# The sample gates of a hybrid decoder step: products with ones in place of a transpose and selection products

## What is computed

```python
g_nsa = jax.nn.sigmoid(nsa_g.reshape(bsz, t, N_HEADS, 3))
o_nsa = jnp.einsum('bthk,btkhd->bthd', g_nsa, o_br).reshape(bsz, t, Q_DIM)
```

## Time and profile before

| | us |
|---|---|
| median of 3 runs | 2087.87 |
| fastest and slowest of them | 2085.74, 2093.57 |
| span of the profiled execution | 2092.6 |
| TensorE busy in it | 2026.6 |
| VectorE, ScalarE, GpSimd busy | 425.8, 323.0, 115.4 |

### The profile page before, as it was taken

One profiled execution on the slowest core, in us unless ns is written; L12 is line 12 of the kernel. 1 busy time (PEld: TensorE's weight loads), 2 busy tenths in 40 slices (PEclk: granted clock), 3 DMA queues, 4 the chain that ended last, 5 costly groups with the idle time before them and its releaser, 6 DMA issues.

```text
span 2092.6 us, 40370 instructions
## 1 busy us (share of the span) xinstructions
PE 2026.6 (97%) x17044; PEld 1201.8 (57%) x17044; DVE 425.8 (20%) x1129; ACT 323.0 (15%) x852; POOL 115.4 (6%) x215
## 2 busy tenths in 40 slices
PE   8998999999999999899999999999999999999996
PEld 6776677777777778567777443343434343434332
DVE  1234365210000132437431300000000000000001
ACT  2243221110000123522211110000101000001010
POOL 2210121000000010120000000000000000000000
PEclk9999999999999999999999999999999999999998
DMA  8852653334333364453333699999999999999996
GB/s 321 301 197 97 209 183 142 141 121 141 136 126 141 118 222 154 150 202 132 116 122 121 259 419 404 414 384 417 378 421 392 409 392 408 390 409 390 408 396 258
DMA packets 98441, 551.25 MB, mean 263 GB/s; under 512 B 12992, under 2 KB 29408, under 8 KB 39520
## 3 DMA queue, kind: packets, MB, share of 16 engines
q1 hardware_dynamic: 84144, 492.75, 60.5%
q0 software_dynamic: 12112, 48.93, 6.6%
q10 hardware_dynamic: 2016, 7.08, 0.9%
HBM read 532.84 MB, written 22.13 MB: 265 GB/s over the span
## 4 chain that ended last, share of the span: by engine, by line
PE 52%; issue 43%; DVE 2%; ACT 1%; DMA 1%; POOL 1%; POOLq 0%; DVEq 0%; SPq 0%
PE bank L463 41%; PE bank L594 3%; PE bank L624 1%; PE bank L649 1%; ACT phase_region L1216 1%; PE bank L841 1%; PE bank L711 1%; PE bank L733 1%; PE bank L777 0%; DVE phase_region L1612 0%; POOL xn L1193 0%; PE bank L637 0%; PE bank L482 0%; PE bank L474 0%; PE bank L563 0%
## 5 line engine op out<-in xcount | busy, mean ns | idle before, releaser
L982 PE MATMUL bank<-wring,phase_region 128*32 128x512 f32 (+2 forms) x9728 | 871.1, 519 | 3.0 <-DMA wring<-in_wstream 2.0
L463 PE MATMUL bank<-xn,wring 128*128 128x288 f32 x2496 | 643.6, 418 | 5.7 <-DVE phase_region L1612 3.6
L982 PEld LDWEIGHTS bank<-wring,phase_region 128*32 128x32 f32 x9728 | 311.5, 110 | 557.4 <-issue 510.3
L463 PEld LDWEIGHTS bank<-xn,wring 128*128 128x128 f32 x2496 | 481.5, 195 | 148.3 <-issue 10.9
L1216 ACT ACTIVATE phase_region<-bank 128x384 f32<-128x384 f32 (+14 forms) x244 | 87.9, 442 | 420.2 <-PE bank L947 205.3
L463 PE MATMUL bank<-phase_region,wring 128*128 128x288 f32 x608 | 148.2, 407 | 3.1 <-DVE mark L1540 2.5
L463 PEld LDWEIGHTS bank<-phase_region,wring 128*128 128x128 f32 x608 | 115.3, 190 | 36.0 <-DVE mark L1540 3.4
L2085 DVE TENSOR_TENSOR tmp<-phase_region,bank 128x512 f32<-128x512 f32 x32 | 22.0, 687 | 531.5 <-PE bank L982 531.5
L1494 ACT ACTIVATE phase_region<-bank 128x512 f32<-128x512 f32 (+1 forms) x48 | 25.2, 543 | 524.7 <-PE bank L982 524.7
L2098 DVE COPY phase_region<-bank 32x256 f32<-32x256 f32 x32 | 13.4, 420 | 297.5 <-PE bank L982 297.2
L594 PE MATMUL bank<-pages,wring 128*64 128x128 f32 (+1 forms) x1024 | 58.9, 276 | 0.0
(11 more groups left out here) (332 smaller groups left out, 1145.7 us busy)
## 6 DMA issues: line engine op xcount, KB each, us to landing
wring<-in_wstream SPq DMA_DIRECT2D x449, 1024.0 KB, 7.7
pages<-in_cmp_pages POOLq DMA_DIRECT2D x64, 128.0 KB, 3.7
pages<-in_cmp_pages SPq DMA_DIRECT2D x64, 128.0 KB, 3.6
pages<-in_slc_pages SPq DMA_DIRECT2D x64, 128.0 KB, 4.6
pages<-in_slc_pages POOLq DMA_DIRECT2D x64, 128.0 KB, 4.6
out_win_keep<-in_win_rows POOLq DMA_DIRECT2D x2, 4064.0 KB, 26.1
y_rows<-phase_region ACTq DMA_DIRECT2D x18, 384.0 KB, 8.1
pages<-in_win_kT POOLq DMA_DIRECT2D x4, 1024.0 KB, 5.3
```

The source lines that it names most:

```text
L463: mm = nc.tensor.matmul(ps[:, 0:width], wb, rhs(k), start=(k == 0), stop=(k == n - 1))
L982: mm = nc.tensor.matmul(ps[QT * q:QT * q + QT, 0:n], lhsT, w, start=start, stop=stop)
```

## The change

The constant `gate_sel` goes, and with it 1536 columns of the constants. The transpose, its bank, its copy on ScalarE and the signal `gT_ready` go. In their place VectorE, right after the norm of the layer and ahead of the rotation, waits for `gates_ready` and makes `gX` in the area of `o_ssm`, which is free at that time. For each group g it is one multiplication: 32 partitions (token t'), 384 columns (branch k, r, token t), the value being the gate (k, r) of token t' where t = t' and zero elsewhere, which is the gate times an identity. TensorE, at the old place of the twelve products, multiplies `gX[:, g]` with a 32 x 64 block of ones into partition half g: the sum over t' leaves the gate of token t on all 64 partitions. These are two matmuls of 384 columns. The copy to `gB` (L1299) and everything behind it stay as they are.

```diff
--- before.py
+++ after.py
@@ -132,12 +132,6 @@
     c["stack"] = (i[:, None] % QT == np.arange(QT)[None, :]).astype(np.float32)
     c["before"] = (i[:, None] < i[None, :]).astype(np.float32)
     c["exp_rank"] = np.broadcast_to(NE - np.arange(NE, dtype=np.float32), (P, NE))
-    sel = np.zeros((P, 12, P), np.float32)
-    for br in range(3):
-        for r in range(GRP):
-            for g in range(NKV):
-                sel[(g * GRP + r) * 3 + br, br * GRP + r, g * HD:(g + 1) * HD] = 1
-    c["gate_sel"] = sel.reshape(P, -1)
     return c
 
 
@@ -227,8 +221,8 @@
         vtok = ra(3, 3, P)
         gates = ra(3, 24)
         small = ra(3, 32)
-        gT = ra(TS)
         gB = ra(3, GRP, TS)
+        gX = view(oS_, 0, NKV, 3 * GRP * TS)
 
         kvT = [(ra(HALF, NCS), ra(HALF, NCS)), (view(oC_, 0, HALF, NCS), view(oC_, HALF * NCS, HALF, NCS))]
         kcTp, vcTp = ra(NCP + 1), ra(NCP + 1)
@@ -340,7 +334,7 @@
         pg_full = [sem(f"pg_full{i}") for i in range(6)]
         names = ("const_in par_in tables_in x_in0 x_in1 ptab_in sq_ready xn_ready x_ready small_ready gates_ready qkv_ready qksq_ready "
                  "inv_ready qkinv_ready rot_in0 rot_in1 rot_cos qk_ready vtok_ready vcT_ready vc_ready smax exp_ready norm_ready pt_ready "
-                 "qbd_ready scmax sc_exp pc_ready ptc_ready ssmax ss_exp pts_ready orow_ready gT_ready attn_done "
+                 "qbd_ready scmax sc_exp pc_ready ptc_ready ssmax ss_exp pts_ready orow_ready gX_ready attn_done "
                  "st_in xbcc_raw xbcc_ready cols_ready spa sp_exp ea_ready dD_ready eb_ready seg_ready dec_exp "
                  "dec_ready tl_sub tl_ready cp_ready xdt_ready btok_ready h_ready bm_ready y_ready ysq_ready "
                  "oS_ready part_sum merged_ready cnt_ready pick_ready table_ready zero_ready "
@@ -524,16 +518,12 @@
                 mm.then_inc(done, 1)
                 for i in range(2, 5):
                     product(("in", l, i), KD, lambda k: xn[:, k, :])
-                pe.wait_ge(S["gates_ready"], l + 1)
-                ps, done = bank(("gT", l))
-                nc.tensor.transpose(ps[0:24, 0:TS], gates[0:TS, 2, :], C("ident", TS)[:, 0:TS]).then_inc(done, 1)
                 for i in range(5, 8):
                     product(("in", l, i), KD, lambda k: xn[:, k, :])
-                pe.wait_ge(S["gT_ready"], l + 1)
+                pe.wait_ge(S["gX_ready"], l + 1)
                 ps, done = bank(("gB", l))
-                for j in range(12):
-                    mm = nc.tensor.matmul(ps[:, j * TS:(j + 1) * TS], C("gate_sel", 24)[:, j * P:(j + 1) * P],
-                                          gT[0:24, :], start=True, stop=True)
+                for g in range(NKV):
+                    mm = nc.tensor.matmul(ps[HD * g:HD * g + HD, 0:3 * GRP * TS], C("ones", TS)[:, 0:HD], gX[0:TS, g, :], start=True, stop=True)
                 mm.then_inc(done, 1)
                 product(("in", l, 8), KD, lambda k: xn[:, k, :])
                 ps, done = bank(("qkss", l))
@@ -1288,10 +1278,6 @@
                 A.activation(gates[:, 0:2, :], small[:, 0:2, 0:24], ACT.Sigmoid).then_inc(S["gates_ready"], 1)
                 for i in range(2, 5):
                     qkv_tile(i)
-                act.wait_ge(*filled(("gT", l)))
-                ps = bank_of(("gT", l))
-                copy(gT[0:24, :], ps[0:24, 0:TS]).then_inc(free(("gT", l)), 1)
-                signal("gT_ready")
                 for i in range(5, 8):
                     qkv_tile(i)
                 act.wait_ge(*filled(("gB", l)))
@@ -1565,6 +1551,13 @@
                 rms(l, 0, "norm_mix")
                 if l == 0:
                     dve.wait_ge(S["tables_in"], 16)
+
+                dve.wait_ge(S["gates_ready"], l + 1)
+                for g in range(NKV):
+                    mine = gates[0:TS, 2, 12 * g:12 * g + 12].rearrange("p (r k) -> p k r", k=3)
+                    one = bc(bc(C("ident", TS)[:, 0:TS], 1, GRP), 1, 3)
+                    last = V.tensor_tensor(gX[0:TS, g, :].rearrange("p (k r t) -> p k r t", k=3, r=GRP), bc(mine, 3, TS), one, ALU.mult)
+                last.then_inc(S["gX_ready"], 1)
 
                 for part, (i0, i1) in enumerate(ROT_PARTS):
                     dve.wait_ge(S[("rot_in0", "rot_in1")[part]], 64 * (l + 1))
```

## The result

| | before | changed |
|---|---|---|
| median of 7 runs, us | 2087.87 | 2080.32 |
| lowest and highest | 2085.58, 2093.83 | 2078.38, 2084.82 |
| span of the profiled execution | 2092.6 | 2077.7 |
| mean granted clock in it | 0.983 | 0.987 |

The ratio is 0.996, with a 95% interval of 0.9947 to 0.9972: 7.6 us of 2087.9, 0.36%. The forecast was 2080.0 us, within 0.5% of before.

A forecast was written before the change was run, and what follows sets the result against it. TensorE, busy for 2026.6 of 2092.6 us, was taken to bound the kernel. Savings of 4.5 us of work and 3.4 us of clock sum to 7.9 us: 2087.9 - 7.9 = 2080.0 us, range 2074 to 2086.

The forecast's parts named there:

- The new products: On TensorE, two matmuls of 384 columns a layer replace the twelve of L535: 0.68 us for 2.79 us.
- the rule by columns from L649: L649's 0.91 us for 512 columns, scaled to 384 columns, prices the two new matmuls at 0.68 us.
- the bound for serial halves: If the bank's two halves do not run beside each other, the new matmuls take 1.29 us a layer.
- The transpose: L529 on TensorE is removed: 0.13 us a layer, 0.26 us in all.
- The product behind: The TensorE product after L535, 7.05 and 5.76 us before, would take 3.95 us like the three before it.
- The clock: TensorE's clock falls at L535 go with it: 3.4 us, bounds zero and 5.1 us.
- VectorE: Two added multiplications a layer ahead of the rotation, 0.54 us each, hidden in idle time: cost nothing.
- What is late next: Behind L543, the reciprocal (L1578) moves forward with TensorE's earlier arrival, 4.1 us margin before L563; gain kept to the end.
- The table: Constants at L1066 lose 768 KB, later loads land some 2.1 us earlier; taken at nothing, bounds 0 and -2.1 us.
- B: Rival: clock falls are not L535's doing and stay, only 4.5 us go: 2083.4 us; chance 0.17.
- C: Rival: all 5.12 us of clock return plus 1.71 us in a later stretch, 11.3 us: 2076.6 us; chance 0.21.
- D: Rival: VectorE's multiplications push the rotation and TensorE waits, 10.3 us a layer: 2100.7 us; chance 0.02.

The follow-up runs named there:

- e2: Changed kernel with twelve small matmuls (24 rows, 128 output partitions, 32 columns) as filler ahead of the two new products in each layer; 2091.77 us.
- e3: Changed kernel with five large matmuls (128 rows, 128 output partitions, 336 columns) as filler ahead of the two new products in each layer; 2087.37 us.
- e8: Kernel before with VectorE's two multiplications added ahead of the rotation, TensorE waiting for them, their result unused; 2087.78 us, ratio 0.9996.
- e7: Changed kernel with VectorE's two multiplications behind the rotation instead of ahead of it; 2102.63 us, ratio 1.0063.
- e12: Changed kernel with the state space branch's small sample-chunk matmuls taken apart by existing products, no work added; 2076.79 us, ratio 0.9945 to the kernel before.
- e10: Changed kernel with twenty-four of the small 32-column matmuls ahead of the two new products in each layer; 2103.90 us.

## Why the prediction held, point by point

**The new products.** Forecast 0.68 us, measured 0.79; the rule by columns from L649 was 0.11 us short, and the bound for serial halves, 1.29, was far off. The transpose is the term mis-sized the other way: 0.32 us a layer for 0.13. Together 2 x (2.00 + 0.32) = 4.6 us for 4.5, two small errors that offset, which is luck. The full-clock part of the runs fell by 5.2 +- 0.4; the 0.6 us beyond 4.6 may be the table, or the error of the split. The product behind takes 4.08 us, not the 3.95 that the prediction took from the mean of three: 4.08 is what the first product behind other work takes here (as at 20.56 us).

**The clock.** Forecast 3.4 us, one loss of 1.71 a layer; measured 2.8 +- 1.1, and rather 2 over all runs of before. The mechanism, that the low clock belongs to L535, is shown by e2 against e3. Its size was a choice between 3.4 and 5.1 us that one profile could not settle. The profiles of e2 and e8 show one loss of 1.7 us in each layer at this place, as the forecast took; that of before showed two in layer 0. The mean of the runs, 2.8 +- 1.1, fits 3.4 well and 5.1 less well. The prediction compared the span of the profiled execution with device times; in the runs whose span is listed the device time is some 2 us longer than the span, so that execution was even longer against the median than the 4.7 us taken. Two readings beside this were not exact, and no term hangs on them. The clock fell nearer to 51.2 than to 51.4 us (0.62 over one microsecond holds 0.76 us at 0.50). And L535 is not the one stretch with 32 columns behind weight loads of 128: L523 is another, with six instructions in 0.54 us, and the clock does not fall there.

**A reading that was wrong.** I put all of 35.6 us of missing clock down as lost. About 7 of them are the end of the program, where TensorE has nothing to do; the clock is low there and costs nothing. It changed no term of the sum, since the low stretches at L535 had TensorE busy.

**VectorE.** 0.54 us forecast and measured, hidden as forecast (e8), with the cover worth 14.2 us of waiting and 5.8 us of slower products if it is gone (e7).

**What is late next.** Nothing was: the reciprocal (L1571, L1578 before) moved with its input by 5.61 us in layer 0, with 0.61 us of idle time left before it of 6.01. It ends at 59.37 us and L553 starts at 63.48, the margin of 4.1 us that was forecast. No wait appears before L553, the line of L563 in the changed kernel; TensorE waited for weights 2.1 us in all, for 2.0 before.

```profile
...
56.07 3.30 DVE L1571 RECIPROCAL phase_region<-phase_region 128x504 f32<-128x504 f32 x1 [0.61 <-ACT phase_region L1289]
```

**The table.** Taken at nothing; the runs allow for nothing to about 1 us (0.4 +- 0.4 of work).

**The rivals.** B fell with e2 and e3: had only the work gone, 2083.4 us, but the medians were 2080.3 and 2080.2. C took place in the pair of profiled executions (14.9 us apart, 6.6 of them from stretches that the change does not touch), but not in the medians. D did not occur.

The errors of the two terms, work 0.7 us too low and clock 0.6 us or more too high, offset each other; the total of 7.6 against 7.9 is closer than its parts. The second error lies within that of its measurement (2.8 +- 1.1).

## What to carry to other kernels

Price a group of small matmuls not only by its own time but also by the product behind it: compare that product with its equals elsewhere in the chain, and then read the granted clock of the stretch. To tell cause from luck, replace the suspected matmuls by large ones of the same total time; where the cause is confirmed, try existing large work between the small ones, as in e12. And compare kernels by many runs, splitting the time by the mean clock; two profiles alone can differ by twice the effect. Lost clock counts only where TensorE had work: take out the stretches in which it stood still.

## What the runs showed of the hardware

The granted clock fell to 1.2 GHz behind stretches in which TensorE was busy without a gap, with 24 or 48 instructions of 32 columns (e2, e10), and not behind ten instructions of 336 columns in the same time (e3). Twelve small matmuls (2.8 us) did so at some places only: 4.6 +- 1.2 us over two places behind product 7, but 4.4 +- 2.2 us over twelve places elsewhere. Twenty-four in a row did so in both layers of the profile, and cost 10.3 +- 1.1 us of clock in the mean (e10). Which place falls stays open, and so does which part of the shape counts. Once low, the clock stayed at 0.50 through 32 instructions of 64 rows and 256 columns (L831, 6.8 us, TensorE busy without a gap); with whole products put in between (e12) it was at 1.00 through the same instructions. One multiplication by VectorE of 32 x 384 elements, both operands broadcast, took 0.54 us, close to the line between 0.45 us for 288 elements and 0.69 for 512.
